# Seven block products for the gate and value tiles of the two FFNs

## The reference

```python
def conv_ffn(h, w_up, conv_w, conv_b, w_down):
    u = h @ w_up                                   # (1024, 1024) @ (1024, 2 * 2816)
    u = lax.conv_general_dilated(                  # causal, 3 taps, each channel by itself
        u, conv_w[:, None, :].astype(u.dtype), window_strides=(1,),
        padding=[(CONV_WIDTH - 1, 0)], dimension_numbers=('NWC', 'WIO', 'NWC'),
        feature_group_count=u.shape[-1]) + conv_b
    gate, val = jnp.split(u, 2, axis=-1)
    return (jax.nn.silu(gate) * val) @ w_down      # (1024, 2816) @ (2816, 1024)

for layer in range(DEPTH):
    ...
    x = x + rmsnorm(a, g_attn_post[layer])
    h = rmsnorm(x, g_ffn_pre[layer])
    f = conv_ffn(h, ffn_w_up[layer], ffn_conv_w[layer], ffn_conv_b[layer], ffn_w_down[layer])
    x = x + rmsnorm(f, g_ffn_post[layer])
```

## Time and profile before

| | us |
|---|---|
| median of 3 runs (2773.2 to 2776.72) | 2773.89 |
| the profiled execution | 2778.58 |
| its span in the trace | 2776.6 |
| PE busy | 2576.6 |
| DVE busy | 1407.1 |
| POOL busy | 881.6 |
| ACT busy | 782.4 |

### The profile page before, as it was taken

The page is one execution under the profiler, slowest core; times in us unless marked ns, Lnnn a source line. Parts: engine busy times, 40 slices in busy tenths (PEclk is TensorE's granted clock), DMA queues, the critical chain, the costliest instruction groups (busy, mean ns, idle before and its releaser), DMA issues.

```text
span 2776.6 us, 32261 instructions
## 1 busy us (share of the span) xinstructions
PE 2576.6 (93%) x12444; PEld 2072.7 (75%) x12444; DVE 1407.1 (51%) x1641; ACT 782.4 (28%) x1337; POOL 881.6 (32%) x619
## 2 busy tenths in 40 slices
PE   7899999899999999997799999979799999999994
PEld 4688888578888888884577787757488888888883
DVE  4476674653333333336767677653743333333337
ACT  3344441221111111113346565551321111111111
POOL 4222112453333333333531323112553333333332
PEclk9999999999999999998999999979899999999997
DMA  3121133011111111111211312032011111111111
GB/s 130 49 76 64 62 113 130 30 38 46 46 54 46 45 53 45 45 53 48 91 50 43 92 46 76 24 144 98 23 44 48 46 49 50 45 48 51 45 45 61
DMA packets 44436, 166.19 MB, mean 60 GB/s; under 512 B 5552, under 2 KB 6064, under 8 KB 40880
## 3 DMA queue, kind: packets, MB, share of 16 engines
q1 hardware_dynamic: 36592, 132.14, 14.9%
q10 hardware_dynamic: 7744, 32.66, 3.0%
HBM read 129.65 MB, written 20.97 MB: 54 GB/s over the span
## 4 chain that ended last, share of the span: by engine, by line
PE 79%; DVE 12%; ACT 4%; DMA 1%; issue 1%; SPq 1%; POOL 1%; ACTq 0%; POOLq 0%; DVEq 0%
PE ps L893 11%; PE ps L894 11%; PE ps L895 11%; PE ps L914 6%; PE ps L915 5%; PE ps L916 5%; PE ps L789 3%; PE ps L687 3%; PE ps L689 3%; PE ps L688 3%; PE ps L761 2%; DVE a L1290 2%; PE ps L763 2%; PE ps L762 2%; PE ps L826 2%; PE ps L806 2%
## 5 line engine op out<-in xcount | busy, mean ns | idle before, releaser
L893 PE MATMUL ps<-h,w_hi 128*128 128x512 f32 x1408 | 551.0, 391 | 8.5 <-POOL h L567 7.7
L894 PE MATMUL ps<-h,w_hi 128*128 128x512 f32 x1408 | 549.2, 390 | 0.0
L895 PE MATMUL ps<-h,w_lo 128*128 128x512 f32 x1408 | 549.2, 390 | 0.0
L1503 DVE SCALAR_TENSOR_TENSOR tg<-ps,cv,tg 128x1023 f32<-128x1023 f32 x88 | 112.9, 1283 | 799.4 <-ACT tg L1205 799.4
L548 POOL TENSOR_TENSOR w_lo<-w_raw,w_hi 128x1024 fp32r<-128x1024 f32 x194 | 469.0, 2418 | 15.6
L546 POOL CAST w_hi<-w_raw 128x1024 fp32r<-128x1024 f32 x194 | 204.9, 1056 | 790.4 <-PE ps L763 275.8
L1205 ACT ACTIVATE tg<-ps,cv 128x1024 f32<-128x1024 f32 x88 | 106.3, 1208 | 994.2 <-PE ps L895 994.2
L545 POOL TENSOR_TENSOR gate<-ones 128x1 f32<-128x1 f32 x120 | 23.4, 195 | 945.7 <-PE ps L895 520.2
L893 PEld LDWEIGHTS ps<-h,w_hi 128*128 128x128 f32 x1408 | 265.2, 188 | 70.0 <-POOL h L567 13.2
L895 PEld LDWEIGHTS ps<-h,w_lo 128*128 128x128 f32 x1408 | 265.2, 188 | 55.3
L894 PEld LDWEIGHTS ps<-h,w_hi 128*128 128x128 f32 x1408 | 265.3, 188 | 54.5
(11 more groups left out here) (176 smaller groups left out, 4435.4 us busy)
## 6 DMA issues: line engine op xcount, KB each, us to landing
w_raw<-in_W SPq DMA_DIRECT2D x194, 512.0 KB, 3.3
h<-o_dram ACTq DMA_DIRECT2D x2, 6144.0 KB, 21.1
dsw<-draw SPq DMA_DIRECT2D x64, 128.0 KB, 2.3
o_dram<-most SPq DMA_DIRECT2D x6, 1024.0 KB, 4.2
o_dram<-dost SPq DMA_DIRECT2D x6, 1024.0 KB, 4.6
x<-in_x ACTq DMA_DIRECT2D x8, 512.0 KB, 9.8
x<-in_x ACTq DMA_DIRECT2D x1, 4096.0 KB, 12.9
x_dram<-x ACTq DMA_DIRECT2D x2, 2048.0 KB, 7.2
```

The source lines that it names most:

```text
L893: pe.matmul(out, wh, xh, start=k == 0, stop=False)
L894: pe.matmul(out, wh, xl, start=False, stop=False)
L895: last = pe.matmul(out, wl, xh, start=False, stop=k == KT - 1)
```

## The change

For each unit the product of the 2x2 blocks (gate and value tile; lower and upper 512 features; first and second 512 tokens) is computed with seven block products in place of eight, in the form with 4 sums of weight blocks, 4 of token blocks and 7 of results.

- **TensorE** runs, for each unit, the products P1 P6 P2 P5 P7 P4 P3, each of 4 blocks x 3 = 12 matmuls into one bank out of four (0 to 3, in turn), and behind them the whole down product of the unit before: 8 tiles of 6 matmuls. It waits for the weights item by item (`item_ready`). At the very end stands the down product of the last unit.
- **POOL** prepares nine items of 512 columns for each unit, each with a cast and a subtraction, into a ring of five slots, and forms the four sums of weight blocks S1, S3, S2 (`sums`) and S4 (`last_sum`). Slot 0 holds G1, then the first half of the down weights d1; slot 3 holds S1, then d2.
- **DVE** adds seven results (`result`) of 512 columns out of PSUM into `cx` in SBUF, and the convolution now reads `cx` and `cy`, both in SBUF (`conv_tile`, two instructions to a tile; `product` and `hid_tail` stay as they were). The eight adds of the down product stand in one run. The value tile's taps come ahead of C12, the gate tile's behind the adds.
- **ACT** copies P1 out of its bank (`bank_copy`) and takes the newest tap from `cx`.
- Ahead of the stage, `blocks` (DVE), `cast` (ACT) and POOL form the token blocks and their combinations T1 to T4, each cast and subtracted, 28 tiles of 512 columns in all. Two combinations lie over x, which is therefore written out before and read back at the end.
- The hardware loops of this stage are gone; its instructions stand in the program one by one.

The core of the diff:

```diff
+PRODUCTS = ["P1", "P6", "P2", "P5", "P7", "P4", "P3"]
+FIRST_PRODUCTS = ["P1", "P2", "P5", "P6", "P7", "P4", "P3"]
+WEIGHT_OF = {"P1": "G1", "P2": "G2", "P6": "S2", "P7": "S3", "P5": "S1", "P4": "V2", "P3": "S4"}
+TOKENS_OF = {"P1": "B11", "P2": "B21", "P6": "T2", "P7": "T3", "P5": "T1", "P4": "T4", "P3": "B22"}
+RING_SLOT = {"G1": 0, "S2": 1, "G2": 2, "S1": 3, "S3": 4, "d1": 0, "V2": 1, "S4": 2, "d2": 3}
...
+ITEMS = ["G1", "S2", "G2", "S1", "S3", "d1", "V2", "S4", "d2"]
...
+RESULT_OF = {"P6": "U2", "P2": "C11", "P5": "W", "P7": "U3", "P4": "C21", "P3": "C12"}
...
+        cx = at("cx", 42, 4)
+        hid = at("hid", 42, 4, F32R)
+        cy = at("cy", 46, 2)
...
+                def item(n, name, free):
+                    at_ = ring[RING_SLOT[name]]
+                    count = item_count(layer, n, name)
+                    pool.wait_ge(free[0], free[1])
+                    pool.tensor_copy(half_of(at_, 0, 0), raw[name]).then_inc(item_hi, 1)
+                    pool.wait_ge(item_hi, count)
+                    pool.tensor_tensor(half_of(at_, 0, 1), raw[name], half_of(at_, 0, 0).bitcast(F32), ALU.subtract
+                                       ).then_inc(item_ready, 1)
...
+                def sums(n):
+                    count = 4 * (HT * layer + n)
+                    loaded("V", n)
+                    pool.tensor_tensor(raw["S1"], half_of(w_raw, 1, 0), raw["V2"], ALU.add).then_inc(w_sum, 1)
+                    pool.wait_ge(w_sum, count + 1)
+                    pool.tensor_tensor(raw["S3"], raw["G1"], half_of(w_raw, 1, 0), ALU.subtract).then_inc(w_sum, 1)
+                    pool.wait_ge(w_sum, count + 2)
+                    pool.tensor_tensor(raw["S2"], raw["S1"], raw["G1"], ALU.subtract).then_inc(w_sum, 1)
+                    pool.wait_ge(w_sum, count + 3)
+                def last_sum(n):
+                    pool.tensor_tensor(raw["S4"], raw["G2"], raw["S2"], ALU.subtract).then_inc(w_sum, 1)
+                    pool.wait_ge(w_sum, 4 * (HT * layer + n) + 4)
...
+                item(0, "G1", before[0])
+                item(0, "G2", before[0])
+                norm_help(2 * layer + 1, tails=False)
+                sums(0)
+                item(0, "S1", before[1])
+                item(0, "S2", before[1])
+                item(0, "S3", before[1])
+                for k in range(KH):
+                    pool.wait_ge(b_t1, KH * layer + k + 1)
+                    b12, b22 = half_of(a, k, 1), half_of(a, KH + k, 1)
+                    pool.tensor_tensor(b12, b22, b12, ALU.subtract).then_inc(b_t3, 1)
+                for k in range(KH):
+                    pool.wait_ge(b_t2, KH * layer + k + 1)
+                    pool.wait_ge(b_lo_dve, len(TAILS_DVE) * layer + TAILS_DVE.index(("B21", k)) + 1)
+                    b21 = half_of(a, KH + k, 0)
+                    pool.tensor_tensor(b21, b21, half_of(cy, k // 2, k % 2), ALU.subtract).then_inc(b_t4, 1)
+                item(0, "V2", up_of(0, "P6"))
+                for k in range(KH):
+                    tail("T4", k)
+                last_sum(0)
+                item(0, "S4", up_of(0, "P2"))
+                for k in range(KH):
+                    tail("B22", k)
+                for n in range(1, HT):
+                    loaded("G", n)
+                    item(n, "G1", up_of(0, "P1") if n == 1 else down_of(n - 2, 3))
+                    sums(n)
+                    item(n, "S2", up_of(n - 1, "P4"))
+                    item(n, "G2", up_of(n - 1, "P3"))
+                    item(n, "S1", up_of(0, "P5") if n == 1 else down_of(n - 2, 7))
+                    item(n, "S3", up_of(n - 1, "P7"))
+                    loaded("D", n - 1)
+                    item(n, "d1", up_of(n, "P1"))
+                    item(n, "V2", up_of(n, "P6"))
+                    last_sum(n)
+                    item(n, "S4", up_of(n, "P2"))
+                    item(n, "d2", up_of(n, "P5"))
+                loaded("D", HT - 1)
+                item(HT, "d1", down_of(HT - 2, 3))
+                item(HT, "d2", down_of(HT - 2, 7))
...
+                def up(n, place, product):
+                    at_ = ring[RING_SLOT[WEIGHT_OF[product]]]
+                    out = up_bank(n, product)
+                    pe.wait_ge(item_ready, item_count(layer, n, WEIGHT_OF[product]))
+                    bank_free(n, place - 4)
+                    for k in range(KH):
+                        c = TOKENS_OF[product]
+                        if n == 0 and (c, k) in TAILS_DVE:
+                            pe.wait_ge(b_lo_dve, len(TAILS_DVE) * layer + TAILS_DVE.index((c, k)) + 1)
+                        elif n == 0:
+                            pe.wait_ge(b_lo_pool, len(TAILS_POOL) * layer + TAILS_POOL.index((c, k)) + 1)
+                        wh, wl = at_[:, 0, k * P:(k + 1) * P], at_[:, 0, HB + k * P:HB + (k + 1) * P]
+                        _, xh, xl = combination(c, k)
+                        pe.matmul(out, wh, xh, start=k == 0, stop=False)
+                        pe.matmul(out, wh, xl, start=False, stop=False)
+                        last = pe.matmul(out, wl, xh, start=False, stop=k == KH - 1)
+                    last.then_inc(up_done, 1)
...
+                def down(n, f):
+                    part = f // 4
+                    at_ = ring[RING_SLOT[("d1", "d2")[part]]]
+                    if f % 4 == 0:
+                        pe.wait_ge(item_ready, item_count(layer, n + 1, ("d1", "d2")[part]))
+                        pe.wait_ge(hid_lo, u0 + n + 1)
+                    if n > 0 or f >= 2:
+                        pe.wait_ge(acc_done, down_count(layer, n, f) - 2)
+                    f4 = f % 4
+                    wh, wl = at_[:, 0, f4 * P:(f4 + 1) * P], at_[:, 0, HB + f4 * P:HB + (f4 + 1) * P]
+                    for half in range(2):
+                        out = bank(4 + 2 * (f % 2) + half)
+                        xh, xl = half_of(hid, 2 * (n % 2), half), half_of(hid, 2 * (n % 2) + 1, half)
+                        pe.matmul(out, wh, xh, start=True, stop=False)
+                        pe.matmul(out, wh, xl, start=False, stop=False)
+                        last = pe.matmul(out, wl, xh, start=False, stop=True)
+                    last.then_inc(dn_done, 1)
+                for n in range(HT):
+                    for place, product in enumerate(PRODUCTS if n else FIRST_PRODUCTS):
+                        up(n, place, product)
+                    if n:
+                        for f in range(KT):
+                            down(n - 1, f)
+                for f in range(KT):
+                    down(HT - 1, f)
...
+                for n in range(HT):
+                    if n:
+                        bank_copy(layer, n)
+                        gate_and_split(n - 1)
+                    act.wait_ge(c_sum, result_count(layer, n, "C21"))
+                    tap(n, 1)
+                    act.wait_ge(c_sum, result_count(layer, n, "C12"))
+                    if n:
+                        act.wait_ge(hid_lo, u0 + n)
+                    tap(n, 0)
+                gate_and_split(HT - 1)
...
+                def scaled(i):
+                    half, k = NORM_TILES[i]
+                    dve.scalar_tensor_tensor(half_of(a, k, half), half_of(x, k, half), gain(pre, k),
+                                             half_of(rstd_x, 0, half), ALU.mult, ALU.mult).then_inc(b_f, 1)
+                def tail(name, k):
+                    src, hi, lo = combination(name, k)
+                    dve.wait_ge(b_hi, len(CASTS) * layer + CASTS.index((name, k)) + 1)
+                    dve.tensor_tensor(lo, src, hi.bitcast(F32), ALU.subtract).then_inc(b_lo_dve, 1)
+                dve.wait_ge(x_rstd, 2 * n + 1)
+                for i in range(KT):
+                    scaled(i)
+                    if i >= 1:
+                        tail(*TAILS_DVE[i - 1])
+                dve.wait_ge(x_rstd, 2 * n + 2)
+                for k in range(KH):
+                    scaled(KT + k)
+                    scaled(KT + KH + k)
+                    if k == 0:
+                        tail(*TAILS_DVE[KT - 1])
+                    b11, b12, b22 = half_of(a, k, 0), half_of(a, k, 1), half_of(a, KH + k, 1)
+                    dve.wait_ge(b_lo_dve, len(TAILS_DVE) * layer + TAILS_DVE.index(("B11", k)) + 1)
+                    dve.wait_ge(b_f, 2 * KT * layer + SCALED.index(KT + KH + k) + 1)
+                    dve.tensor_tensor(b11, b12, b11, ALU.subtract).then_inc(b_t1, 1)
+                    dve.wait_ge(b_t1, KH * layer + k + 1)
+                    dve.tensor_tensor(half_of(cy, k // 2, k % 2), b22, b11, ALU.subtract).then_inc(b_t2, 1)
+                    if k >= 1:
+                        tail("T1", k - 1)
+                tail("T1", KH - 1)
+                for c in ("T2", "T3"):
+                    for k in range(KH):
+                        tail(c, k)
...
+                def result(n, name):
+                    g, v = cx[:, 2 * (n % 2), :], cx[:, 2 * (n % 2) + 1, :]
```

(37 more changed lines are left out.)

364 lines of the change are left out of this document (186 added, 178 removed).

## The result

| | before | after |
|---|---|---|
| median, us | 2775.2 (2773.2 to 2776.72) | 2923.67 (2922.28 to 2927.99) |
| runs | 4 | 4 |
| span of the profiled execution | 2776.6 | 2921.2 |

The changed kernel is slower by a ratio of 1.0538, 95% interval 1.052 to 1.0556. The forecast was 2904 in a range of 2812 to 2945.

A forecast was written before the change was run, and what follows sets the result against it. TensorE bounds the kernel before; after the change POOL's circle sets a unit. One FFN: 59.3 + 26.4 + 20 x 33.7 + 51.5 = 811.2 against 746.2, twice 65.0 more; time 2904 us, range 2812 to 2945.

The forecast's parts named there:

- The circle: Per unit, POOL's list from G1 to S4, P3, then four down tiles: 30.1 us, 33.7 with hold-ups; main case, 0.66.
- hold-ups: Four 1024-column DVE instructions with two SBUF operands per unit each delay POOL some 1.0 us, 3.6 in all.
- signs that the prediction named for the middle of an FFN: TensorE idle about 1 us and less before P4 and P3; POOL busy 26 to 27 us, then waiting some 7.
- DVE's chain alone: Rival: hold-ups fall beside POOL's waiting or are shorter; unit 31.8, FFN 772.5, time 2827 us; chance 0.17.
- No hold-ups at all: Rival: start 43 + 23.5, unit 31.7, end 51.3, FFN 752, time 2785 us; chance 0.05.
- The start: Unit 0 of an FFN, preparing token blocks on DVE and POOL: 59.3 us; P6 ends at 594.4, unit 0 at 613.6.
- V2's item: At the FFN's start, a step on POOL alone behind P6: 2.1 us.
- four subtractions of B22: At the FFN's start, on POOL: 5.1 us, held up 2.9 by DVE's T3 and results.
- The end: Behind the last unit's P3: last down block begins after 21.7 us, its tiles and squares follow; 51.5 us in total.
- Outside: Writing x out, reading it back, raw weight loads and dropping the loops were costed at nothing.
- break-even unit of 31.4: Faster case (TensorE stays the bound, 0.06) decides from this unit downwards: (746.2 - 43 - 23.5 - 51.3) / 20.

The follow-up runs named there:

- Experiment 1: Changed kernel with DVE's gate-tile taps, product and split reading a PSUM bank for one of two SBUF operands (wrong data): 2822.85 us.
- 2: Changed kernel without POOL's four sums of weight blocks in every unit but the first (work left out): 2824.55 us.
- kernel 6: Changed kernel with down tiles and their adds moved between products: two after P7, two after P4, four after P3: 2793.99 us.
- 11: As kernel 6, but ACT instead of POOL casts one item of a unit, S2: 2765.15 us, ratio 0.9974 to the kernel before.
- 3: Changed kernel with both the PSUM operand for DVE's gate taps, product and split and no weight sums after the first unit: 2819.13 us.
- kernel 9: As kernel 7, but DVE adds the fourth down tile (f 3) before the value tile's taps: 2890.81 us, ratio 1.0431 to the kernel before.
- 10: As kernel 6, but DVE adds the fourth down tile (f 3) before the value tile's taps: 2855.91 us, ratio 1.0305 to the kernel before.
- kernel 7: As kernel 6, and ACT instead of POOL makes the casts of units 1 to 21: 2802.1 us, ratio 1.0112 to the kernel before.

## Why the prediction was right, and where it was off

**The circle** was right as a mechanism and in its pieces. Forecast: 20.8 for POOL's list, 3.6 of hold-ups, 9.3 for P3, four tiles and semaphores. Measured: 20.94, 3.73 and 9.36. A cast of 512 columns takes 0.61 and not 0.56, but starts 0.05 before the last subtraction's end, so that an item stands at 1.94 as forecast; a sum follows the last at 1.37 and not 1.34. Such small terms make the 0.35 us a unit by which the forecast fell short, 14 us in 40 units. The signs that the prediction named for the middle of an FFN are there too (P4 and P3 waiting 1.01 and 0.27, POOL busy for 26.6 us and then idle for 7.43); a third wait for the ring, 0.52 ahead of P2, it did not name. Experiments 1 and 2 shorten the list by 3.7 and by 5.5 us and both end at the chain below it, and 6 takes the circle's closing tile out of its place with the list unchanged; so that this circle set the unit is shown from three sides.

**The hold-ups** were taken from rows of 1024-column instructions as 1.0 each, less for gaps. They are 1.00 for a cast and 0.86 for a subtraction. The prediction had no row in which a cast held DVE up. It can happen: the tap at 816.72, with POOL's cast ending at 817.16, takes 1.51 in place of 1.28. It is DVE's time, and DVE was not on the circle, as the prediction had it.

**DVE's chain alone** was a rival at 31.8 a unit and 772.5 an FFN. Experiment 1, with these hold-ups gone and nothing else, gives 31.8 and 772.8. The rival named the floor below the forecast right; what it assumed, that hold-ups fall beside POOL's waiting, was not so. "No hold-ups at all" had nearly the same unit (31.7) and a start and end shorter by 19 us; it fell with the rows of 2.15 and 1.61.

**The start** came out as the sum said, 59.3, in both halves: P6 ended 40.0 us behind P1's start where 40.1 was forecast, the rest took 19.3 and not 19.2. Here the closeness is partly luck. From DVE's first scaling (539.79) to its last subtraction for T2 it took 43.2 where 42.2 was forecast (14 steps of 1.1 make 15.4, and the sum used 15.8), and P6 ended 1.0 behind that and not 1.8:

```profile
577.28 5.72 DVE L1473 TENSOR_TENSOR t_r<-cy,t_r 128x512 fp32r<-128x512 f32 x4
```
```profile
583.74 0.39 PE L1064 MATMUL ps<-t_r,ring 128*128 128x512 f32 x1
```

In the second half V2's item took 2.8 and not 2.1, and the four subtractions of B22 7.0 where they and their hold-ups had 8.0. TensorE's granted clock from 543 to 604 was 0.69, with waits of up to 5.98 us, which the sum had not asked about; it cost little, since TensorE waited for the others.

**The end** is the term that was mis-sized most for one part: 51.5, measured 55.7. One of two taps was taken as held up. Both were, the second by 1.5, because POOL begins the next stage's weights with an instruction of 2.88 us there (L636), so that the last down block began 1.3 late (23.0 behind P3 and not 21.7, where the terms named add up to 21.8). Its first tile reached its add in 2.9 us and not 1.8, at the granted clock of 0.50 behind the wait of 10.73, which the sum did not ask about. And two of the adds of squares take 2.18 and 2.15 for 1.23, 1.9 together.

**Outside** the FFNs nothing was forecast, and some 10 us came back, by luck against the two FFNs' 24.1 above their forecast. The trace has them ahead of the first FFN's start; what gave them was not tried. The two FFNs took 154.1 us more and not 130.0; less 9.5 outside, that is 14.6 above the forecast span. The other 5 us of the miss are the step from one execution to the median: the one profiled before was 4.7 above the median of the three runs then known, the one after is not above its own (2921.2 + 2.0 against 2923.67).

**Where the saving went.** The change takes 22 x 12 x 0.228 = 60 us of matmuls off an FFN. The faster version of it (11) gains 20 x (32.9 - 30.34) = 51 of them in its units, and still its FFN 0 is 745.1 to 746.2 before. The rest, units 0 and 1 and the end, is 745.1 - 20 x 30.34 = 138 where before had 746.2 - 20 x 32.9 = 88: 50 given back. The start makes and waits for the token blocks, and at the end a whole down block waits for the last gate tile, once an FFN. The prediction's break-even unit of 31.4 took a short start; with the measured start and end it is (746.2 - 142.3) / 20 = 30.2, and so even a TensorE that never waits barely wins. By the traces the two FFNs of 11 are shorter by 1.2 and 1.7; the rest of its 5.7 us lies outside them, and no run shows where it comes from.

## What to carry to other kernels

- A busy share below one does not say that an engine has room. Look for the circle: which of its steps waits for the result of another engine's last step, and how long is the list between the two. Moving the step that closes the circle ahead of other work gave more (130 us, kernel 6) than lightening the engine itself (99 to 105 us, kernels 1 to 3), since the latter stopped at the next chain.
- When work moves into SBUF so that PSUM comes free, list which other engine reads SBUF at that time. A reordering that brings two such streams together can cost more than the wait it removes (9, 10).
- For a form that has fewer products but a preparation of its own, work out start and end first; here they took back 50 of the 51 us that the units of an FFN gained.

## What was not expected of the hardware

- TensorE's clock can fall inside a steady stage: after a wait of 1.82 us (kernel 9) the granted clock was 0.57 over 4 us and eight matmuls came at 0.43, its lower level (1.2 GHz); after a wait of 1.81 in the next unit it stayed at 1.00. Of 40 such waits it fell after 28. Waits up to 1.01 (changed kernel) left it at 1.00 from 700 to 1000 us.
- POOL's casts are held up as much as its subtractions (1.61 for 0.61, 2.15 for 1.29), by DVE instructions with two SBUF operands and not by those with one in PSUM.
- ACT's casts of the same 512 columns show no hold-up. These are those of kernel 7 that read the raw weights, ns min/median/max:

```profile
L1419 ACT ACTIVATE ring<-w_raw x252: 612/619/637, 610.3 to 2714.6; 128x512 fp32r<-128x512 f32 x126
```
